# Low halves of the weights on VectorE in two attention stages, GpSimd resting there

## The reference, cut to what matters

```python
def diff_attention(h, pos, w_qkv, ...):          # first block, 8 heads
    qkv = h @ w_qkv
    q, k = rms_norm(...), rms_norm(...)
    sc = einsum(q, k) * scale + bias_of_distance  # two maps per head
    wts = softmax(sc0) - lam * softmax(sc1)
    o = rms_norm(wts @ v) * (1 - lam_init)
    return o @ w_o

def mla_attention(h, pos, w_dq, w_uq, ..., w_o, k_nope, k_pe, v):  # second block, 16 heads
    q = (rms_norm(h @ w_dq) @ w_uq)               # nope and rope parts
    sc = (einsum(qn, k_nope) + einsum(qp, k_pe)) * scale
    return (softmax(sc) @ v) @ w_o
```

## Time and profile before

| what | value |
|---|---|
| median of 3 runs | 2247.43 us (2239.24 to 2249.46) |
| profiled execution, its time | 2244.81 us |
| its span, first to last instruction | 2243.1 us |
| TensorE busy | 2190.5 us, 98% |
| VectorE / ScalarE / GpSimd busy | 1267.0 / 939.3 / 817.2 us |
| mean granted TensorE clock | 0.997 |

### The profile page before, as it was taken

How to read it: one execution, slowest core, us unless ns; L and a number is a source line. 1 busy time by engine, 2 the same in 40 slices (tenths; PEclk the granted TensorE clock), 3 DMA queues, 4 the chain that set the end, 5 groups by cost and what they waited for, 6 DMA issues and landing times.

```text
span 2243.1 us, 25847 instructions
## 1 busy us (share of the span) xinstructions
PE 2190.5 (98%) x9992; PEld 1712.5 (76%) x9992; DVE 1267.0 (56%) x2181; ACT 939.3 (42%) x1544; POOL 817.2 (36%) x320
## 2 busy tenths in 40 slices
PE   7999999999999999999999999999998999999998
PEld 4777688888887667768888888887774588888887
DVE  5876665554247688773655562276957643333224
ACT  5666543433233566653333332232227632222224
POOL 3222344444444222113444444434320144444432
PEclk9999999999999999999999999999999999999999
DMA  8121323333222111102333332344310033333222
GB/s 279 57 66 43 95 93 103 94 95 112 91 95 79 69 48 38 43 29 94 94 94 101 97 108 91 101 138 147 113 57 20 29 94 99 98 94 112 91 98 85
DMA packets 58793, 200.99 MB, mean 90 GB/s; under 512 B 6608, under 2 KB 10208, under 8 KB 58672
## 3 DMA queue, kind: packets, MB, share of 16 engines
q1 hardware_dynamic: 56816, 196.78, 27.5%
q10 hardware_dynamic: 1856, 2.57, 0.4%
HBM read 197.19 MB, written 7.38 MB: 91 GB/s over the span
## 4 chain that ended last, share of the span: by engine, by line
PE 85%; DVE 9%; DMA 2%; ACT 2%; issue 1%; SPq 1%; POOL 0%; DVEq 0%; ACTq 0%
PE lin L522 24%; PE lin L523 23%; PE lin L524 23%; DVE arena L1678 2%; PE obank L834 1%; PE scores L812 1%; PE turn L638 1%; PE scores L816 1%; PE lin L556 1%; DMA a_bias_by_distance<-a_bias_rows 1%; PE obank L715 1%; PE lin L557 1%; PE lin L558 1%; PE scores L1029 1%; PE scores L672 1%
## 5 line engine op out<-in xcount | busy, mean ns | idle before, releaser
L2463 POOL TENSOR_TENSOR w_lo<-slots,w_hi 128x1024 fp32r<-128x1024 f32 (+4 forms) x314 | 814.1, 2595 | 1401.6 <-ACT w_hi L1953 1390.8
L1953 ACT ACTIVATE w_hi<-slots 128x1024 fp32r<-128x1024 f32 (+4 forms) x314 | 349.2, 1112 | 605.3 <-DMA slots<-in_w_ffn_in 278.3
L522 PE MATMUL lin<-g_hi,w_hi 128*128 128x512 f32 x1408 | 552.5, 392 | 0.0
L524 PE MATMUL lin<-g_hi,w_lo 128*128 128x512 f32 x1408 | 548.0, 389 | 0.0
L523 PE MATMUL lin<-g_lo,w_hi 128*128 128x512 f32 x1408 | 547.9, 389 | 0.0
L522 PEld LDWEIGHTS lin<-g_hi,w_hi 128*128 128x128 f32 x1408 | 264.3, 188 | 63.0 <-issue 7.6
L523 PEld LDWEIGHTS lin<-g_lo,w_hi 128*128 128x128 f32 x1408 | 264.3, 188 | 56.0 <-issue 1.7
L524 PEld LDWEIGHTS lin<-g_hi,w_lo 128*128 128x128 f32 x1408 | 264.3, 188 | 54.9
L1214 DVE TENSOR_TENSOR h<-lin,h 128x512 f32<-128x512 f32 x72 | 49.7, 691 | 307.1 <-PE lin L524 297.9
L522 PE MATMUL lin<-f_hi,w_hi 128*128 128x512 f32 x528 | 205.4, 389 | 0.0
L523 PE MATMUL lin<-f_lo,w_hi 128*128 128x512 f32 x528 | 205.4, 389 | 0.0
(11 more groups left out here) (459 smaller groups left out, 3493.9 us busy)
## 6 DMA issues: line engine op xcount, KB each, us to landing
slots<-in_w_ffn_in SPq DMA_DIRECT2D x132, 512.0 KB, 3.5
slots<-in_w_ffn_out SPq DMA_DIRECT2D x48, 704.0 KB, 4.0
slots<-in_w_ple SPq DMA_DIRECT2D x24, 640.0 KB, 3.8
slots<-in_w_a_qkv SPq DMA_DIRECT2D x24, 512.0 KB, 3.6
slots<-in_w_c_in SPq DMA_DIRECT2D x23, 512.0 KB, 3.5
slots<-in_w_b_wo SPq DMA_DIRECT2D x16, 512.0 KB, 3.5
slots<-in_w_b_pair SPq DMA_DIRECT2D x8, 768.0 KB, 4.1
slots<-in_w_a_wo SPq DMA_DIRECT2D x16, 256.0 KB, 2.6
```

Source lines behind the costliest of these rows:

```text
L522: pe.matmul(bank[:, parity, :], hi, x_hi, start=k == 0, stop=False)
L524: mm = pe.matmul(bank[:, parity, :], lo, x_hi, start=False, stop=k == len(rhs) - 1)
L1953: ac.activation(w_hi[:, slot, at_], slots[:, slot, at_], ACT.Copy).then_inc(q.hi_made, 1)
L2463: po.tensor_tensor(w_lo[:, slot, at_], slots[:, slot, at_], w_hi[:, slot, at_].bitcast(F32), ALU.subtract).then_inc(q.weights_split, 1)
```

## The change

VectorE makes the low halves of groups 3 to 23 of `a_qkv` (21 of 128x1024) and of groups 2 to 15 of `b_pair` (7 of 128x1536 and 7 of 128x1024) with one subtraction each, at places fixed in its order. GpSimd skips these groups, and before each of its own it now also waits for `weights_split` at n, since the counter is raised by two engines. VectorE's `low_half` waits for the count and for the high half.

```diff
+            def low_half(n):
+
+                slot, at_ = ring(n)
+                ve.wait_ge(q.weights_split, n)
+                ve.wait_ge(q.hi_made, n + 1)
+                ve.tensor_tensor(w_lo[:, slot, at_], slots[:, slot, at_], w_hi[:, slot, at_].bitcast(F32), ALU.subtract)\
+                    .then_inc(q.weights_split, 1)
...
+                def low(n):
+                    if RING <= n < 3 * AH:
+                        low_half(GROUP["a_qkv"] + n)
...
-                    lam_and_bias()
+                    lam_and_bias(); low(3)
                 elif proj:
-                    biased(0); square_split(2); take_(0); biased(1); weights_(0); square_split(0); weights_(1)
-                    take_(1); biased(2); lows(); biased(3); square_split(1); weights_(2); weights_(3); out_normed()
+                    biased(0); low(3 * s + 1); square_split(2); take_(0); biased(1); low(3 * s + 2); weights_(0)
+                    square_split(0); weights_(1); take_(1); biased(2); lows(); biased(3); low(3 * s + 3)
+                    square_split(1); weights_(2); weights_(3); out_normed()
                     take_(2); normed(0); normed(1); output(); angles_()
...
+                def low(n):
+                    if 2 <= n < 2 * B_PAIRS:
+                        low_half(GROUP["b_pair"] + n)
...
-                take_(0); take_(1); biased(0); square_split(0); take_(2); square_split(1); take_(3); weights_(0)
+                take_(0); take_(1); low(2 * s + 1); biased(0); square_split(0); take_(2); square_split(1); take_(3); weights_(0)
                 normed(0); biased(1); take_(4); square_split(2); first_half(0); output(0); first_half(1); biased(2)
-                square_split(3); normed(1); weights_(1); first_half(2, 3); take_(5); normed(2); output(1); square_split(4)
+                square_split(3); normed(1); weights_(1); first_half(2, 3); take_(5); normed(2); low(2 * s + 2); output(1); square_split(4)
...
                 slot, at_ = ring(n)
+                if RING <= n < GROUP["a_wo0"] or GROUP["b_pair"] + 2 <= n < GROUP["b_wo0"]:
+                    continue
+                wait(po, q.weights_split, n)
                 po.wait_ge(q.hi_made, n + 1)
```

## The result

The change makes the kernel 0.17% slower: 2250.04 us, median of 20 runs (2246.91 to 2256.90), against 2247.32 for the kernel before in 20 runs (2239.24 to 2252.79). The ratio is 1.0017 with a 95% interval of 1.0009 to 1.0025, so 3.8 us (2.0 to 5.6) on 2247.3. Among the executions of the kernel before that were timed beside the experiments, two far slower ones (2451.8 and 5633.95 us) are left out of every comparison here. The forecast was 2248.7 and "within 0.5% of before"; the measured median lies 1.3 us above the one and inside the other. The profiled execution has a span of 2245.6 us at a mean clock of 0.994.

What follows compares the result with a forecast made beforehand. TensorE, busy 98% of the span, was taken as the bound. The terms +5.4 + 1.3 + 0.35 - 1.8 - 4.0 gave +1.3 us, moving the median from 2247.43 to 2248.7 us, range 2239 to 2260.

Steps and rivals of the forecast that it cites:

- The stall at the seam: Between steps 0 and 1 of the first stage, TensorE waits for `low(3)`: 5.4 us (4.7 to 6.1).
- The clock: Behind the stall before step 1, TensorE's matmuls run at clock 0.50: 1.3 us lost (0 to 2.8).
- I take the same again: Six to seven slow matmuls, seen behind earlier gaps before 230.94, assumed again behind the stall before step 1: 1.3 us.
- Rival 1: Before step 1, the clock doesn't fall or `low(3)` is reached sooner: 2247.4 or 2243.5 us; chance 0.2.
- `low(4)`: In step 1 of the first stage nothing covers this low half, so lin_(1) starts 0.35 us later (0 to 1.2).
- Score banks: First stage: TensorE's waits for emptied score banks vanish except step 1's, 1.8 us won of 3.3.
- The second stage: TensorE's waits for the squares' low half and the output copy shrink: 4.0 us won (2.5 to 6.8).
- Hidden, barely at the first: First stage, steps 2 to 7: `low(3s + 2)` ahead of `take_(1)` costs nothing, 1.23 us against 1.55 idle.
- rival 2: VectorE's order becomes the bound, decided at `low(3s + 2)`: 2263 us, or 2294 with all low halves uncovered; chance 0.06.
- The sum: Whole kernel: all terms together add 1.3 us (bounds -3.9 to +5.8), so the median becomes 2248.7 us.
- 3: Both stages: VectorE's stalls are not GpSimd's doing and the change doesn't free VectorE: 2266 us; chance 0.04.
- 4: Both attention stages: the seam is covered and all TensorE gaps go, 13.7 us won, 2234 us; chance 0.03.

Runs made afterwards that it cites:

- the two kernels without it: Against the changed kernel: GpSimd still makes group 3's low half, 2242.43 us; or VectorE makes it behind `take_(1)` of step 0, 2241.93 us.
- the kernel with the shorter stall: Changed kernel with `low(3)` between step 0's three small operations and the register load and branch; 2250.62 us, 1.0018 of before.
- second stage alone: Changed kernel, but GpSimd keeps all low halves of the first stage; 2243.27 us, 0.9985 of before.
- the doubled kernel: Changed kernel with a second, value-preserving VectorE operation after each first-stage low half from group 5 on, 19 in all; 2252.72 us, 1.0026 of before.
- GpSimd's idle reads: Changed kernel; GpSimd subtracts constants into an unused buffer at the moments of the old first-stage low halves; 2256.37 us, 1.0047 of before.
- first stage alone: Changed kernel, but GpSimd keeps all low halves of the second stage; 2254.70 us, 1.0039 of before.
- `low(3)` early: Changed kernel with `low(3)` behind `take_(1)` in step 0 instead of at the end of the step; 2241.93 us, 0.9980 of before.

## Why the prediction was right, point by point

*The stall at the seam.* Forecast +5.4 us (4.7 to 6.1); TensorE started 41.80 - 36.56 = 5.2 us later. The parts: the small operations ended at 39.3, not 40.0; the load and the branch took 1.26 us, not 0.8, near the upper bound of 1.31; the subtraction 1.22. The first part has a reason that the prediction overlooked: step 0 had a stall of its own, beside GpSimd's low half of group 3. First GpSimd and VectorE before, then VectorE after:

```profile
31.55 2.46 POOL L2463 TENSOR_TENSOR w_lo<-slots,w_hi 128x1024 fp32r<-128x1024 f32 x1 [3.80 <-ACT w_hi L1953]
...
32.39 1.91 DVE L1372 TENSOR_SCALAR arena<-arena 128x511 f32<-128x511 f32 x1
```
```profile
32.52 0.42 DVE L1372 TENSOR_SCALAR arena<-arena 128x511 f32<-128x511 f32 x1
```

With it gone, VectorE's order of step 0 ends 0.7 us sooner. That the load and the branch lie on the path was shown by moving `low(3)` ahead of the load (1.2 us less stall), and that the seam holds the loss by the two kernels without it.

*The clock.* Forecast 6.5 slow matmuls, 1.3 us; there were nine, 1.8 us. The step "I take the same again" from another stall was the weak one: 9 to 11 behind 5.7 us, 12 and 8 in the kernel with the shorter stall. At the seam it stayed inside 0 to 2.8 us in the changed kernel's profile, but not in that one, with 4.0 us; for the whole kernel the timed runs put it above 2.8 as well, as the sum below tells. Rival 1's condition, that the clock doesn't fall, is not met.

*`low(4)`.* Forecast 0.35 us; the row at 52.83 shows 0.22.

*Score banks.* Forecast -1.8; from 3.3 to 1.4 us, -1.9.

*The second stage.* Forecast -4.0 (2.5 to 6.8). The two waits of TensorE fell from 6.6 to 3.4 and from 2.6 to 1.8, together 4.0; C to D fell by 4.1 to 4.7; the timed second stage alone gives -3.4 (1.3 to 5.4). All three are one answer within their scatter.

*What was wrong though it cost nothing:* "Hidden, barely at the first" for `low(3s + 2)`, and with it rival 2's "decides from 0.3 us of misjudgement". The slack was read off VectorE's idle time ahead of `take_(1)`; the doubled kernel put another 1.23 us there and lost some 1.4 us over the stage (one profile). The chance of that rival should have been smaller, and its point of decision over a microsecond further on.

*The sum.* With the measured terms: 5.2 + 1.8 + 0.2 - 1.9 - 4.0 = +1.3 us, as forecast, by errors that cancel (0.2 less stall, 0.5 more clock). The measured difference is 3.8 us (2.0 to 5.6): the forecast of +1.3 lies below the interval. The sum is therefore too small by 0.7 us or more, and that it agrees with its own measured terms is in part luck.

The rest is most likely slow matmuls away from the seam. The record has the mean granted clock of each timed execution, for the kernel before in 86 executions beside the experiments and for the changed one in its 20:

| mean granted clock | before: executions, mean time | changed: executions, mean time |
|---|---|---|
| 0.996 to 0.998 | 54, 2245.5 us | none |
| 0.995 | 18, 2249.6 us | 3, 2248.8 us |
| 0.994 | 11, 2250.0 us | 8, 2248.8 us |
| 0.993 | 3, 2250.7 us | 4, 2251.1 us |
| 0.991 and 0.992 | none | 5, 2254.1 us |

Where the clocks are equal, 0.993 to 0.995, the two kernels take the same: 2249.8 and 2249.4 us. The changed kernel's clock is lower, 0.9934 on average against 0.9959, and within either kernel 0.001 of it goes with 1.7 to 2.0 us. As an estimate from these figures, the clock term is 2.5 x 1.7 to 2.5 x 2.0, or 4.3 to 5.0 us, where the prediction had 1.3 (0 to 2.8). The other measured terms give 5.2 + 0.2 - 1.9 - 4.0 = -0.5 us, so the sum comes to 3.8 to 4.5, and 3.8 was measured. The term that was mis-sized is then the clock's. Of it 1.8 us are read at the seam; the rest lies elsewhere, at places that differ from profile to profile. This is a relation between runs and not shown by an experiment: none held the clock fixed, and the two kernels' executions in the table were not timed side by side. The other kernels go with it: the first stage alone has a clock of 0.9944, 1.5 steps of 0.001 down, some 3 us, and with its terms of 5.2 + 0.2 - 1.9 = 3.5 that is 6 to 7 of the measured 8.8 (5.6 to 11.9); the kernels without the long stall have most of their clock back: 0.9956 with group 3 on GpSimd, 0.9953 with `low(3)` early, 0.9962 for the second stage alone.

What profiles say of the rest is less. By the ratios the first stage alone costs 8.8 us (5.6 to 11.9) and leaving group 3 to GpSimd gains 8.5 on the changed kernel; by mark A of the profiles they are 4.7 and 6.4 us, and the two stages' marks together, +4.7 - 4.7, would make no difference at all. Behind mark D every kernel runs the same instructions, and yet that part differs by some 7 us from profile to profile, 1188.5 to 1195.9 us, with no order by kernel. It holds stretches at the clock of 0.5 at other places each time: by windows of 5 us none with the first stage alone, 7 us in both profiles of before, 10 after and 17 with the second stage alone. One profile each can't tell a small later effect of the first stage from this scatter.

*Rivals.* 1 fell with the clock's row, 2 with the doubled kernel, 3 with GpSimd's idle reads. 4, more of the idle time goes, did not happen in the changed kernel, and is true in part once the seam is mended: with `low(3)` early the kernel is 4.5 us faster than before, of the 13.7.

## What to carry to other kernels

Work moved to a busier engine is paid for only where it meets an empty moment of the critical engine's order: here 33 of 35 subtractions held TensorE up nowhere, one cost it 0.2 us, and one, placed behind a chain of small operations, a register load and a branch, lost more than all the others had won. Check the first round of a pipeline by itself, since the cover of the settled rounds isn't there yet. And measure slack from the consumer, by when the next instruction that needs the result would start, not from the producer's idle time; with the two buffers here it is a tile longer.

Where a difference is some tenths of a per cent, take the granted clock of each run beside its time, and profile the unchanged kernel twice before reading one stage's length off it.

## What the hardware showed unexpectedly

- A VectorE operation on 128x1 stands still like a large one while GpSimd works: 2.23 us in the earlier trace rows and 1.75 us beside GpSimd's 1.89, against 0.16 us alone. So does one with a single tensor as input (line 1372: 1.91 against 0.42 us). The stall shows as a longer instruction, not as a wait, so a sum of busy time hides it.
- A register load with its branch on VectorE: 1.26 us of "issue", on the path.
- The granted clock doesn't answer to the nearest stall alone. Behind a stall of 5.7 us 9 to 11 matmuls were slow in three profiles; behind one of 4.45 us 12, and 8 more some 6.5 us later, behind a gap that left the clock up elsewhere; behind one of 2.02 us none at once, but seven or eight were some 6 us later, behind another of 1.4 us that the changed kernel also has. At one place what a stall costs by way of the clock was known here to some 2 us, no better; over the whole kernel the timed runs suggest 4 to 5 us for a change whose seam shows 1.8.
